# Expert gather in groups of two slots instead of four

## The reference

```
h = rmsnorm(x); proj = h @ w_in                     # q, k, v and three inputs of a gated conv
x = x + concat(rmsnorm(stick_breaking_attention(q, k, v)), rmsnorm(gated_conv)) @ w_out
xn = rmsnorm(x)
per token, per head of 8:                           # PEER: product-key retrieval
  s1, s2 = (xn @ wq) against 2 x 128 keys           # top 16 of each, top 16 of the 256 sums
  idx, g = 16 expert numbers, softmax of their scores
  act = gelu(xn . u_tab[idx])                       # u_tab, v_tab: 16384 x 1024
  x = x + sum(g * act * v_tab[idx])
out = rmsnorm(x)                                    # 1024 tokens, width 1024
```

## Time and profile before

| | before |
|---|---|
| time, median of 3 | 3310.59 us (3310.36 to 3325.57) |
| the profiled execution: time | 3309.24 us |
| the profiled execution: span from first to last instruction | 3307.5 us |
| TensorE busy, share | 2376.0 us, 72% |
| VectorE busy, share | 2463.9 us, 74% |
| ScalarE busy, share | 908.8 us, 27% |
| GpSimd busy, share | 1372.8 us, 42% |
| moved by DMA | 1212.75 MB, of which 1073.81 MB in GpSimd's queue; mean 367 GB/s |

### The profile page before, as it was taken

How to read it: one execution, slowest core, us unless ns; L and a number is a source line. 1 busy time by engine, 2 the same in 40 slices (tenths; PEclk the granted TensorE clock), 3 DMA queues, 4 the chain that set the end, 5 groups by cost and what they waited for, 6 DMA issues and landing times.

```text
span 3307.5 us, 27587 instructions
## 1 busy us (share of the span) xinstructions
PE 2376.0 (72%) x7364; PEld 1293.4 (39%) x7364; DVE 2463.9 (74%) x5342; ACT 908.8 (27%) x2063; POOL 1372.8 (42%) x1296
## 2 busy tenths in 40 slices
PE   8669896689888795776878877677577555554554
PEld 7547463256554352333544433244233222221221
DVE  1665779867898699776678887689865577777776
ACT  2132512421665111232116644212111211111111
POOL 0132333333444333444444544444444355554553
PEclk9879998899889897887989899888798777777777
DMA  6879698899888998999999999999999999999997
GB/s 229 331 300 354 259 381 340 337 383 408 342 333 336 361 387 331 368 369 372 418 419 367 395 371 371 404 419 402 367 382 373 366 396 398 398 397 387 391 403 320
DMA packets 185029, 1212.75 MB, mean 367 GB/s; under 512 B 20672, under 2 KB 20672, under 8 KB 53440
## 3 DMA queue, kind: packets, MB, share of 16 engines
q0 software_dynamic: 147456, 1073.81, 81.4%
q1 hardware_dynamic: 37440, 137.40, 10.8%
HBM read 1198.54 MB, written 12.58 MB: 366 GB/s over the span
## 4 chain that ended last, share of the span: by engine, by line
PE 30%; DMA 25%; DVE 22%; issue 14%; ACT 6%; POOL 2%; SPq 0%; POOLq 0%; DVEq 0%; ACTq 0%
DMA ring<-in_uv,cur_idx 22%; PE vacc L938 12%; DVE ring L1113 9%; PE bank L976 6%; DVE acc L1133 4%; PE bank L1044 3%; POOL ring L716 2%; PE o_ps L942 2%; DMA xn<-in_final_norm_g 1%; ACT L734 1%; PE bank L972 1%; ACT diag L759 1%; DVE lt L1250 1%; DVE ocT L1260 1%; PE bank L987 1%
## 5 line engine op out<-in xcount | busy, mean ns | idle before, releaser
L938 PE MATMUL vacc<-ring,diag 128*128 128x512 f32 x1884 | 1175.3, 766 | 827.3 <-ACT diag L759 826.8
L716 POOL DMA_INDIRECT ring<-in_uv,cur_idx x1024 | 1219.6, 1191 | 957.6 <-PE vacc L938 342.8
L1113 DVE CUSTOM_DVE_ANT_0 ring<-ring,xn 128x1024 f32<-128x1024 f32 x1024 | 1223.3, 1221 | 431.8 <-DMA ring<-in_uv,cur_idx 426.8
L938 PEld LDWEIGHTS vacc<-ring,diag 128*128 128x128 f32 x1884 | 442.9, 247 | 1454.5 <-ACT diag L759 951.4
L1133 DVE SCALAR_TENSOR_TENSOR acc<-ring,g_w,acc 128x512 f32<-128x512 f32 (+1 forms) x844 | 678.3, 804 | 35.2
L755 ACT ACTIVATE g_ge<-dots 128x4 f32<-128x4 f32 x256 | 52.5, 205 | 1852.7 <-DVE dots L1113 1843.5
L707 POOL COPY cur_idx<-idx 128x4 uint32<-128x4 uint32 (+1 forms) x256 | 151.1, 590 | 947.8 <-DVE acc L1133 765.3
L759 ACT ACTIVATE diag<-ident,g_w 128x128 f32<-128x128 f32 x942 | 302.8, 390 | 79.5 <-DVE g_w L1122 79.5
L976 PE MATMUL bank<-hT,wpool 128*128 128x256 f32 (+2 forms) x1280 | 285.0, 382 | 1.4 <-ACT hT L786 1.4
L976 PEld LDWEIGHTS bank<-hT,wpool 128*128 128x128 f32 x1280 | 219.7, 192 | 69.6 <-issue 12.9
L1055 PE MATMUL bank<-hT,wpool 128*128 128x256 f32 (+2 forms) x1024 | 235.9, 386 | 2.2 <-ACT hT L868 2.2
(11 more groups left out here) (129 smaller groups left out, 1574.0 us busy)
## 6 DMA issues: line engine op xcount, KB each, us to landing
wpool<-in_w_in SPq DMA_DIRECT2D x96, 512.0 KB
wpool<-in_peer_wq SPq DMA_DIRECT2D x64, 512.0 KB
wpool<-in_w_out SPq DMA_DIRECT2D x32, 512.0 KB
ring<-in_uv,cur_idx POOLq DMA_INDIRECT x1024
xb<-in_x SPq DMA_DIRECT2D x15, 512.0 KB
x_scratch<-xb SPq DMA_DIRECT2D x8, 512.0 KB
xn_scratch<-xb SPq DMA_DIRECT2D x8, 512.0 KB
xn<-xn_scratch SPq DMA_DIRECT2D x8, 512.0 KB
```

What stands on the lines that cost most here:

```text
L716: nc.gpsimd.indirect_dma_start(ring[:, s, :], None, uv, bass.IndirectOffsetOnAxis(ap=cur_idx[:, s:s + 1], axis=0))\
L938: ins = nc.tensor.matmul(vacc[:, :], diag[:, q, s, :], ring[:, q * GROUP + s, D:D + PE_COLS], start=first and s == 0, stop=last and s == G ...
L1113: ins = nc.vector.tensor_tensor_reduce(out=ring[:, s, 0:D], in0=ring[:, s, 0:D], in1=xn[:, c % 2, :], scale=1.0, scalar=0.0, op0=ALU.mult, ...
```

## The change

Groups have two slots in place of four. The ring still has eight slots and is now four groups (`LAP` = 4). Each step done per group is done per pair: gelu on two dots, one weight product of two, one index copy of two numbers. A part 0 or 1 has one dot in place of two. A narrow group gives TensorE 1 of 2 slots in place of 2 of 4. `timeline()` has 64 groups of three parts per chunk in place of 32, so the front's steps are spread over twice as many parts; `EARLY_PARTS` is 2. The positions in a chunk at which other loads are issued are kept in slots, or nearly.

```diff
-GROUP = 4
+GROUP = 2
 GROUPS = SLOTS // GROUP
-EARLY_PARTS = 1
+EARLY_PARTS = 2
 PARTS = 3
-RING = 2 * GROUP
+LAP = 4
+RING = LAP * GROUP
 PE_COLS = 512
-PE_SLOTS_NARROW = 2
+PE_SLOTS_NARROW = 1
...
-            out.append(("body", c, 1, GROUPS // 2 - 2))
-            out.append(("body", c, GROUPS // 2 - 1, 1))
+            out.append(("body", c, 1, GROUPS // LAP - 2))
+            out.append(("body", c, GROUPS // LAP - 1, 1))
...
-                if g == (8 if c + 1 < b else GROUPS - 4):
+                if g == (GROUPS // 4 if c + 1 < b else GROUPS - GROUPS // 8):
                     out.append(("front", "sp", "load_chunk", c + 1))
...
-                if g == 1 and c > 0:
+                if g == GROUPS // 32 and c > 0:
                     out += [("front", "dve", "final_scale", c - 1), ("front", "sp", "store_y", c - 1)]
...
-        diag = sb("diag", [P, 2, GROUP, P])
+        diag = sb("diag", [P, LAP, GROUP, P])
...
-        BODIES = GROUPS // 2
+        BODIES = GROUPS // LAP
...
-                used = (n * 2 + q - 2) * GROUP
+                used = (n * LAP + q - LAP) * GROUP
...
-                    act.wait_ge(s_dot, n * 2 + q + 1)
+                    act.wait_ge(s_dot, n * LAP + q + 1)
                     nc.scalar.activation(g_ge[:, sl], dots[:, sl], ACT.Gelu_apprx_tanh).then_inc(s_gge, 1)
```

More of the change, by code:

```diff
@@ L532, in is_wide @@
         def is_wide(c, i, q):
-            return c in wide_from and 2 * i + q >= wide_from[c]
+            return c in wide_from and LAP * i + q >= wide_from[c]
         def pe_slots(c, i, q):
-            return PE_SLOTS_NARROW if isinstance(i, int) and (c, 2 * i + q) in narrow else GROUP
+            return PE_SLOTS_NARROW if isinstance(i, int) and (c, LAP * i + q) in narrow else GROUP
         def diags_ahead(c, n, i, q):
-            g = 2 * i + q if isinstance(i, int) else GROUPS
-            return (n * 2 + q) * GROUP - (GROUP - PE_SLOTS_NARROW) * sum(1 for e in narrow if e < (c, g))
+            g = LAP * i + q if isinstance(i, int) else GROUPS
+            return (n * LAP + q) * GROUP - (GROUP - PE_SLOTS_NARROW) * sum(1 for e in narrow if e < (c, g))
         def gather_line(eng_group, eng_front, me):
@@ L553, in gather_line @@
                     c, g, part = rest
-                    eng_group(c, g // 2, g % 2, part, g == 0, g == GROUPS - 1)
+                    eng_group(c, g // LAP, g % LAP, part, g == 0, g == GROUPS - 1)
                 else:
@@ L557, in gather_line @@
                     if count == 1:
-                        for q in range(2):
+                        for q in range(LAP):
                             for part in range(PARTS):
-                                eng_group(c, first, q, part, first == 0 and q == 0, first == BODIES - 1 and q == 1)
+                                eng_group(c, first, q, part, first == 0 and q == 0,
+                                          first == BODIES - 1 and q == LAP - 1)
                     else:
@@ L708, in group @@
                     .then_inc(s_idx, 1)
-                pool.wait_ge(s_idx, n * 2 + q + 1)
+                pool.wait_ge(s_idx, n * LAP + q + 1)
                 pool.sem_inc(s_go, 1)
@@ L932, in group @@
                 wide = is_wide(c, i, q)
-                first_wide = wide and 2 * i + q == wide_from[c]
+                first_wide = wide and LAP * i + q == wide_from[c]
                 if first_wide:
@@ L1098, in group @@
                 n = i + c * BODIES
-                G = n * 2 + q
+                G = n * LAP + q
                 sl = slice(q * GROUP, (q + 1) * GROUP)
```

4 lines of the change are left out of this document (2 added, 2 removed).

## The result

The changed kernel takes 3273.36 us (median of 4 runs, 3271.26 to 3275.44) against 3310.48 for the one before (4 runs, 3310.0 to 3325.57): ratio 0.9879, interval 0.9861 to 0.9897, 1.2% faster. The profiled execution took 3273.27 us with a span of 3271.5, against 3309.24 and 3307.5. The forecast took 12 us off the time; 37 came off.

What follows compares the result with a forecast made beforehand. The prediction took gathers to bound chunks 3 to 7, with the DMA partly idle in chunks 0 to 2 and no single engine limiting throughout. Terms: +22 + 4 - 40 + 5 + 0 - 3 = -12, so 3309 - 12 = 3297 us; range 3235 to 3370.

Steps and rivals of the forecast that it cites:

- the likeliest case: Whole kernel: gain and cost cancel, 3275 to 3325 us; chance 0.42.
- Chunks 3 to 7 give nothing, since they already move what the DMA can: Chunks 3 to 7: freeing slots sooner gains 0 us, DMA share being 0.96 to 0.98.
- Part 1: VectorE, twice as many groups at 0.70 us: +22 us in chunks 0 to 2, +4 from 2200 us on, otherwise hidden.
- Part 2: Ring slots come free 2.4 us sooner, closing idle DMA time in chunks 0 to 2: -40 us (bounds 0 and -119).
- rival (c): Chunks 0 to 2: slots wait for TensorE in front work, so nothing is freed sooner; 3337 us, chance 0.12.
- Part 3: ScalarE: 221 table loads in place of 163, mostly covered; +5 us, with 23 if all on the way to gelu showed.
- Part 4: GpSimd: 256 more index copies, about 4.9 us per pair against the DMA's 5.36; no cost (bounds 0 and +40 us).
- rival (b): GpSimd sets the pace at 5.67 us per pair in chunks 6 and 7, +40 us there; 3352 us, chance 0.18.
- Part 5: The rest: TensorE's last burst has 4 matmuls in place of 8, -2.7 us at the end; otherwise 0.
- Rival (a): Chunks 0 to 2: the DMA's holes close, -79 us, with VectorE's extra work mostly hidden (+10); 3237 us, chance 0.28.

Runs made afterwards that it cites:

- gate_freed: The changed kernel, but the first index copy of every two pairs waits until VectorE and TensorE have freed all four slots; 3498.86 us.
- nocopy4: The kernel before (groups of four) without the index copy and its wait, gathers reading `idx` itself, last two chunks' loop written out; 3298.92 us.
- gate_fours: The changed kernel, but the index copy of every first pair of two waits until the adds of three slots are done; 3296.36 us.
- nocopy2: The changed kernel without the index copies, gathers reading `idx` itself, chunks 6 and 7 unrolled; 3277.74 us.
- pairs_old_order: The changed kernel's pairs, with the front's steps in the 32 places per chunk of the kernel before, 219 table loads; 3238.19 us.
- fours_to_c2: The changed kernel with groups of four in chunks 0 to 2 and pairs from chunk 3; 3234.40 us, ratio 0.9779 to the kernel before.
- the mix: Groups of four in chunks 0 and 1, then pairs with front steps in the old 32 places per chunk; 3221.45 us, 0.9725 of the kernel before.

## Why the prediction was right or wrong

3273 lies in the range of 3235 to 3370, but the likeliest case, gain and cost cancelling to within 0.5%, did not come: the kernel is 1.2% faster. The place of both moves was told wrong. For chunks 0 to 2 the sum had -13 and got +38; for 3 to 7 it had +1 (+4 and -3 at the end) and got -74. That the total stayed in the range is luck: two wrong terms had opposite signs.

**The step that failed: "Chunks 3 to 7 give nothing, since they already move what the DMA can".** The term was 0 and measured -74 us. I took a DMA share of 0.96 to 0.98 for the ceiling, though the earlier trace rows had 417 GB/s in one stretch and the earlier trace rows 379 to 394 in those chunks. The same 50 us of chunk 6, before and after:

```profile
2800.00:2850.00 50.00, 28.01 (x40) 10.94 (x40) 38.42 (x63) 7.42 (x25) 24.53 (x22) 0.73 0.99 399
```

```profile
2800.00:2850.00 50.00, 27.82 (x40) 8.96 (x40) 40.65 (x72) 8.98 (x30) 35.38 (x30) 0.77 1.01 422
```

The busy share is the same but for 0.02, the rate 6% higher. One gather is 128 rows of 8 KB, 1.049 MB; at 422 GB/s that is 2.48 us, and 128 of them are 318 us, near the 325.4 of the last stages (2.54 each; before, 2.68).

How a share of 0.98 can leave 5% to gain is in the trace's records of single packets. The share is the time that packets take, and that time is not fixed. In chunk 6, by those records: the time in ns of packets of 8 KB (median, mean, and what 1% of them exceed), the mean busy time of the 16 DMA engines, and the time in which less than one whole gather (128 such packets) was asked for and not yet landed:

| chunk 6 | length | median | mean | 1% over | busy us | short of gathers, us |
|---|---|---|---|---|---|---|
| gate_freed | 367.5 | 309 | 335 | 888 | 350 | 62 |
| before | 343.4 | 309 | 326 | 700 | 338 | 23 |
| nocopy4 | 334.3 | 309 | 320 | 557 | 330 | 19 |
| gate_fours | 328.4 | 312 | 316 | 380 | 329 | 10 |
| nocopy2 | 328.1 | 312 | 314 | 322 | 329 | 7 |
| after | 325.4 | 313 | 314 | 324 | 326 | 7 |

Of the 18 us gained 12 are packets that take less long, which the busy share can't show, and 6 are idle time. The long packets and the time short of gathers go together over the six kernels, and but for the 3 us between the changed kernel and nocopy2 so does the length. Why a packet takes longer where the DMA has run short no run shows.

The earlier trace rows has the pauses of GpSimd, 3.28 us ahead of the copy and 1.67 behind it. After the change the copy follows the gather without a pause:

```profile
2920.15 1.04 POOL L709 COPY cur_idx<-idx 128x2 uint32<-128x2 uint32 x1
...
2922.12 1.09 POOL L718 DMA_INDIRECT ring<-in_uv,cur_idx  x1 [0.93 <-POOL cur_idx L709]
...
2923.51 1.59 POOL L718 DMA_INDIRECT ring<-in_uv,cur_idx  x1 [0.30 <-DVE acc L1135]
2925.12 1.04 POOL L709 COPY cur_idx<-idx 128x2 uint32<-128x2 uint32 x1
```

gate_freed showed that an edit to the moment of the requests moves the rate. What part of the 17 to 18 us per stage comes from smaller portions, and what from the copy no longer standing ahead of four, gate_fours and nocopy4 leave open: the first gave back 3 to 6 us, the second gained 9 and 1.

**Part 1.** Right for chunks 3 to 7: the added turns hide in the waits for landings, which fell from 213.8 to 119.1 and from 108.4 to 39.9 us, 69 us in the last two chunks where 45 were foreseen. The rest may have gone with the faster landings. In chunks 0 to 2 the price of a turn was the wrong one. I priced it by the last stage, where gelu answers in 0.40 us; behind front work it answers up to 14.9 us later. +22 stood for this.

**Part 2.** The 40 us did not come. The stretch that it was read from, after the change:

```profile
350.00:400.00 50.00, 47.14 (x168) 25.72 (x166) 35.18 (x56) 30.41 (x48) 17.60 (x17) 0.90 0.56 204
```

The share went from 0.62 to 0.56. GpSimd's two main waits in this stretch, before and then after:

```profile
POOL cur_idx L707 <- DVE acc L1133: 22.0, 3, 10.5
POOL ring L716 <- PE vacc L938: 12.0, 3, 7.3
```

```profile
POOL ring L718 <- PE vacc L940: 21.9, 4, 7.0
POOL cur_idx L709 <- DVE acc L1135: 10.1, 3, 9.2
```

VectorE's add freed the slots sooner, as forecast, and then they waited for TensorE's matmul, with TensorE busy 47 of the 50 us. That is the mechanism of rival (c). It holds for chunks 0 to 2 as a whole: the waits for an add ahead of the copy fell from 366.4 to 239.6 us, those for the matmul (L938, now L940) rose from 234.4 to 331.8. TensorE in turn waited longer for ScalarE's diagonals there (300.0 us, before 244.2), so ScalarE's late answers are in this too; the traces don't split the two. The rival's 3337 us did not come, for chunks 3 to 7 gained.

**Part 3.** The count of 221 was right. The term of +5 was mis-sized and its bound of +23 too: taking the loads away shortens chunks 0 to 2 by 49 us in pairs and by 8 in fours, so about 41 us of the change's price there hang on loads. I asked what a load adds between a dot and its gelu, and not what the gelu stands behind. The gelu waits of chunks 0 to 2 were foreseen at twice 41 us and are 141.1. Over all stages taking the loads away is worth 73 us in the changed kernel and 14 in the one before (no more than a single total is good to), while pairs_old_order gains 35 us with the loads in place. The page of the Trainium skill that would put a drain of 1.38 us behind every load (ScalarE: Activation LUTs, "What ACT_TABLE_LOAD costs") is not borne out here either: above, gelu starts at 701.89, 0.01 us after the load that began at 700.60 and took 1.28. The load itself began 0.02 us after the activation before it (699.43, 1.15 us).

**Part 4.** Estimated 4.9 us per pair on GpSimd; from one copy to the next above it is 4.97. The agreement is luck: 4.97 is what the DMA needs for two gathers at 422 GB/s, and nocopy2 keeps that pace with 67 us less work on GpSimd. The two ends of the estimate were also not alike (5.67 has the gap of 0.30 to what follows, 4.20 has not), and the 1.67 us that it laid to TensorE's matmul stand in the earlier trace rows as released by VectorE's add. The term, no cost, was right, and rival (b) is refuted by nocopy2 and by the last stages, which got shorter. The page of the Trainium skill on the SBUF's sides (SBUF — State Buffer, "SBUF: two separate sides"), by which a VectorE operation with two SBUF inputs and a GpSimd operation that reads SBUF exclude each other, bears on the duration only: the copy takes 0.73 us in the mean, 1.04 in the rows above against 0.18 undisturbed (at 2905.79 in gate_freed), and twice as many of them cost the last stages nothing.

**Part 5.** TensorE's last burst is down from 5.41 us, by 1.6 and not by 2.7:

```profile
3257.17 3.78 PE L940 MATMUL vacc<-ring,diag 128*128 128x512 f32 x4 [1.99 <-ACT diag L761]
```

**Rival (a)** did not come: chunks 0 to 2, where it placed the gain, got longer. That fours_to_c2 and pairs_old_order reach 3234 and 3238, near its 3237, is chance, since they get there without closing the holes of chunks 0 and 1.

## What to carry to other kernels

Before you call a stage bound by the DMA, compare its GB/s with the best stretch of the same trace, not its busy share with 1; then look whether the queue of transfers runs short between the pauses of the engine that asks for them. When a group is cut in two, look up in each engine's order what now stands between the request to another engine and the wait for its answer: here a round trip that takes 0.4 us alone took up to 14.9 us behind front work. And read the time by stage, since a change can be right for one and wrong for the next, as here, where the mix beats both.

## What the runs showed of the hardware

The DMA engines count as busy at 0.99 while they move 399 GB/s and at 1.01 while they move 422, with the same gathers. The time of a packet of 8 KB varies with how the gathers are asked for: the median was 309 to 313 ns in the six kernels of the table above, but in chunk 6 1% took over 700 ns in the kernel before, over 324 after, and over 888 in gate_freed. The gathers of 1.049 MB go at 2.48 us each (422 GB/s) when they are asked for steadily, and taking 67 of GpSimd's 227 us of work out of a stage (nocopy2) does not change that; in gate_freed the rate of a stage came down to 371 GB/s with the share still at 0.95. A table load of 1.28 us stood between its neighbours on ScalarE with 0.02 us ahead of it and 0.01 behind.
